# Moving the second layer's modulation into the first group's mixing, and giving each mixing step pairs of picks by its stage

## The chip, the cores and the metric

One core of a Trainium2 chip runs the whole inference step in one launch. The metric is the device time of the launch in microseconds (us), median of the runs. Engines are named as in the profile: PE (matmul), PEld (its weight load), DVE (vector), ACT (scalar), POOL (here it only issues the gathers), SP (here it only issues the loads of weights and states).

## The reference

The trunk has two layers over 640 tokens of width 1024 (512 prompt tokens of one sequence, 8 streams of 16 tokens), float32 throughout. Each layer is:

```
mod = silu(c) @ w_mod + b_mod            # 9 conditioning rows (1 prompt, 8 streams), 1024 x 6144 per layer
sh1, sc1, g1, sh2, sc2, g2 = split(mod, 6)
h = rmsnorm(x, ln1_w) * (1 + sc1) + sh1
x = x + g1 * token_mixer(h)              # input projection, SSD scan, RG-LRU, merge, output projection
h = rmsnorm(x, ln2_w) * (1 + sc2) + sh2
x = x + g2 * peer(h)                     # 8 heads x top 16 = 128 experts for each token
```

`peer` picks for each token 128 of 16384 experts by product keys. Each expert is a row u (1024) and a row v (1024): `gelu(u . h) * gate` weights v. So every token needs 128 gathered rows of 8 KB. The modulation depends on the conditioning vectors alone, and layer 1's is first used when layer 1's first normalised input is modulated.

## The kernel before, in words

**Tokens, tiles and groups.** The 640 tokens are 5 tiles of 128. A layer's mixing runs over two groups: tiles 0 to 2 (N = 384 columns) and tiles 3, 4 (N = 256, with the 8 streams). Layer and group make a region r = 0 to 3. A region's mixing is a list of steps i in stages, `bases` gives where each begins: N1 (norm, 12 steps), X (13), S (SSD scan, 19 or 15), Z (8), LX (9), LRU (8), M (merge, 33), OUT (18, with the second norm), Q (queries, key scores and the choice of experts, 21). In a step of X, Z, LX, LRU, M, OUT or Q, PE projects one tile of weights (512 KB, 90 a region, `project`, L460) through 4 slots `wslot` that SP fills in order (`load`, L331). SP waits with each load until the projection that last read the slot is done (`projected`).

**Picks and pairs.** The experts of a tile are gathered one pick at a time: for pick k, POOL gathers a row of 2048 numbers for each of the 128 tokens (1 MB) into one of the 8 places of `ring` (L447). DVE takes the dot product with u (L1726, `dots`), ACT the gelu (L1202), DVE the weight (L1733), ACT a diagonal matrix of the weights (L1182), and PE adds v by that matrix into PSUM (L858, `values`). The place is free when PE is done (`used`). Two picks are a pair, 64 pairs a tile, 640 pairs for the 10 tiles of both layers. The ring holds 4 pairs.

**The plan.** `plan` writes the order of all of it by hand, as a list of slots: a slot is a pair (or none) and the mixing steps that come behind it on PE and DVE (ACT takes the first step ahead of the pair's work). Every engine works through the same list in order. Region 0 has nothing beside it up to step 7 of Q. Then 28 pairs of tile 0 run two to a step, in its Q. `window(pairs, steps, at, till)` lays a region's steps beside the pairs of the layer or group before, evenly: from pair `at` to pair `till` each pair has the same number of steps. Window 1 has region 1 beside the last 36 pairs of tile 0 and those of tiles 1 and 2 (164 pairs, till 151), window 2 has region 2 beside tiles 3 and 4 (128 pairs, steps from 9 to 122), window 3 has region 3 beside tiles 5 to 7 (192 pairs, 9 to 180), and the last 128 pairs have the final norms. With s a tile of a group that already has its scores, `choose` makes the choice for tile s + 1 in 24 pairs of tile s (one of three pieces a pair; the three hold 14 operations over 256 columns for each head).

**Modulation.** A layer's modulation is 12 chunks of 512 columns (2 MB of `w_modt` each). For a chunk PE makes 16 matmul instructions in four column groups (L496), ACT copies the result to `mod_row` (L943), PE turns and sums it (8 instructions, L507), DVE adds the bias into `modE` (L1299). Layer 0's twelve chunks run in N1 and X of region 0, each loaded in one piece to a quarter of the still empty ring (`mod_chunk`). Layer 1's twelve run as a stage MOD of 16 steps at the end of region 1, in window 1, each loaded as four pieces through the four `wslot` slots. PE's chunk there ends with `projected` + 4, so the loads of the next chunk start after it. PE waits for layer 1's modulation (`mod_row`, `mod_add` 24) at the first SSD tile of region 2.

Of the kernel before, what the change touches and what calls it, by code (L numbers as in the profile page):

```python
# [10 lines left out]
DEPTH, D, P = 2, 1024, 128  # L11
# [40 lines left out]
def bases(g):  # L52
    b = {"N1": 0, "X": 12}
    b["S"] = b["X"] + 13
    b["Z"] = b["S"] + (19 if g == 0 else 15)
    b["LX"] = b["Z"] + 8
    b["LRU"] = b["LX"] + 9
    b["M"] = b["LRU"] + 8
    b["OUT"] = b["M"] + 33
    b["Q"] = b["OUT"] + 18  # L60
    b["MOD"] = b["Q"] + 21
    return b
# [3 lines left out]
LENGTH = [BASE[r]["MOD"] + (16 if r == 1 else 0) for r in range(REGIONS)]  # L66
FINAL = 8


def plan():  # L70
# [25 lines left out]
    window(fresh + pairs_of(1, 2), steps_of(1), 0, 64 - 28 + 115)  # L96
# [14 lines left out]
def weight_positions():  # L111

    pos, n = {}, 0
    for r in range(REGIONS):
# [3 lines left out]
        if r == 1:  # L118
            pos[r, "MOD"] = n
            n += 48  # L120
# [51 lines left out]
def build(nc, a):  # L172
    ctx = ExitStack()
    with ctx:
# [143 lines left out]
        mod_row = room(RM - 512, 512)  # L318
# [3 lines left out]
        with nc.Block() as block:  # L322
            @block.sync
            def _(sp):
# [45 lines left out]
                for r in range(REGIONS):  # L370
# [10 lines left out]
                    for j in range(4):  # L381
                        load(tile(l, TZ + j))
                    if g:
                        states(l)
                    for j in range(4, 8):
                        load(tile(l, TZ + j))
# [12 lines left out]
                    if r == 1:  # L399
# [52 lines left out]
            def _(pe):  # L452
# [28 lines left out]
                def modulation(c, in_ring):  # L481

                    if c:
                        pe.wait_ge(S["mod_row"], c)
                    if in_ring:
                        pe.wait_ge(mod_in[c % 4], 16 * (c // 4 + 1))
                    else:
                        for i in range(4):
                            ready(POS[1, "MOD"] + (c - 12) * 4 + i)
                    for kk in range(2):  # L490
                        for q in range(4):
                            if in_ring:
                                w = mod_slab[:, c % 4, (2 * q + kk) * 512:(2 * q + kk + 1) * 512]
                            else:
                                w = wslot[:, (POS[1, "MOD"] + (c - 12) * 4 + q) % SLOTS, kk * 512:(kk + 1) * 512]
                            last = pe.matmul(bank(5)[32 * q:32 * q + 32, :], cT[:, 2 * q + kk, :], w, start=kk == 0, stop=kk == 1)  # L496
                    if in_ring:
                        last.then_inc(S["mod_main"], 1)
                    else:
                        last.then_inc(projected, 4)  # L500

                def modulation_sum(c):
# [3 lines left out]
                    for d in range(4):  # L506
                        last = pe.matmul(bank(6)[:, d * 9:d * 9 + 9], mod_row[:, d * P:(d + 1) * P], pick32[:, 0:9], start=True, stop=True)  # L507
# [59 lines left out]
                def ssd_tile(r, u, i):  # L567
# [7 lines left out]
                    if i == 1:  # L575
# [242 lines left out]
                def mix(r, i):  # L818
# [4 lines left out]
                    if r == 0 and 2 <= i < 6:  # L823
                        modulation_sum(i - 2)
                    if r == 0 and i < 4:
                        modulation(i, True)
                    x_stage(r, i - b["X"])
                    if r == 0 and 2 <= i - b["X"] < 10:
                        modulation_sum(2 + i - b["X"])
                    if r == 0 and 0 <= i - b["X"] < 8:  # L830
                        modulation(4 + i - b["X"], True)
# [8 lines left out]
                    if r == 1 and 2 <= i - b["MOD"] < 14:  # L840
                        modulation_sum(10 + i - b["MOD"])
                    if r == 1 and 0 <= i - b["MOD"] < 12:
                        if i == b["MOD"]:
                            pe.wait_ge(S["p0"], chosen(2))
                        modulation(12 + i - b["MOD"], False)
# [61 lines left out]
            def _(act):  # L907
# [26 lines left out]
                def modulation(c):  # L934
                    if c < 12:
                        act.wait_ge(S["mod_main"], c + 1)
                    else:
                        act.wait_ge(projected, POS[1, "MOD"] + 4 * (c - 11))
# [4 lines left out]
                    act.activation(mod_row, bank(5), ACT.Copy).then_inc(S["mod_row"], 1)  # L943
# [213 lines left out]
                def mix(r, i):  # L1157
# [4 lines left out]
                    if r == 0 and 1 <= i < 5:  # L1162
                        modulation(i - 1)
                    x_stage(r, i - b["X"])
                    if r == 0 and 1 <= i - b["X"] < 9:
                        modulation(3 + i - b["X"])
# [707 lines left out]
```

## Time and profile before

| what | value |
|---|---|
| median of 3 runs | 4863.31 us (4852.66 to 4869.21) |
| the profiled execution's own time | 4843.43 us |
| its span | 4841.7 us |
| mean granted TensorE clock | 0.865 |
| busy share of the span: PE, DVE, ACT, POOL | 76%, 63%, 24%, 30% |
| moved by DMA | 1609 MB, 1342 MB of it by the gathers, mean 332 GB/s |
| first gather issued | 595.4 us |

Slots of the plan are found in the trace by the dot products, four instruction records to a pair (two products, two reads of the accumulator). Region 0 runs to about 783 us, the last part of it beside pairs; window 1 from 783 to 2006 us, window 2 to 3010, window 3 to 4210, and the last pairs to the end. In a table by stretches the number behind each busy time (x...) counts instructions.

| stretch, us | stages | pairs |
|---|---|---|
| 783 to 1016 | region 1: N1, X, S | 39 |
| 1016 to 1222 | Z, LX, LRU | 25 |
| 1222 to 1424 | M | 32 |
| 1424 to 1532 | OUT | 18 |
| 1532 to 1700 | Q | 21 |
| 1700 to 2006 | MOD (16 steps), then pairs alone | 38 |
| 2006 to 2238 | region 2: N1, X, S | 35 |
| 2238 to 2422 | Z, LX, LRU | 20 |
| 2422 to 2643, 2643 to 2740 | M, OUT | 26, 15 |
| 2740 to 2930, 2930 to 3010 | Q, pairs alone | 17, 15 |
| 3010 to 3289 | region 3: N1, X, S | 49 |
| 3289 to 3532 | Z, LX, LRU | 32 |
| 3532 to 3781, 3781 to 3907 | M, OUT | 41, 22 |
| 3907 to 4096, 4096 to 4210 | Q, pairs alone | 27, 21 |

### The profile page before, as it was taken

To read this page: it belongs to the slowest core of one execution; us is meant where nothing else is said; L and a number is where in the kernel's file an instruction comes from. 1 tells how busy PE (TensorE), PEld (TensorE's weight loads), DVE (VectorE), ACT (ScalarE), POOL (GpSimd) and SP (SyncE) were. 2 spreads that over 40 slices of the span, in tenths; PEclk is the share of its full clock that TensorE was granted. 3 is DMA by queue.
4 is the path that set the end of the run, shared out by engine and by line. 5 is a ranking of instruction groups with operands and counts; after the bars stand their busy time and mean duration, and the time that the engine had idled before them with its cause. 6 is when DMAs were issued, how large, how long until landed. Compare 5 with 4: busy or idle time off the path is not lost. (4 is left out here: it accounts for less than half of the span.)

```text
span 4841.7 us, 54018 instructions
## 1 busy us (share of the span) xinstructions
PE 3687.0 (76%) x19330; PEld 1806.0 (37%) x19330; DVE 3049.1 (63%) x8043; ACT 1145.8 (24%) x3125; POOL 1450.5 (30%) x1298
## 2 busy tenths in 40 slices
PE   7999875888987645689999875778788776555555
PEld 4555531444554311144544331334445432111111
DVE  2460289879645923686843596875974478585554
ACT  2150122324212211223411221241431122121111
POOL 0000033332334212423222313343233333444443
PEclk9999987989998867789999987898899887778877
DMA  7133399999999778988888968999999998999997
GB/s 284 48 100 103 102 356 372 379 381 356 378 414 396 295 287 361 387 302 336 310 322 328 346 227 344 369 415 374 356 374 419 401 391 307 398 404 421 407 421 322
DMA packets 275545, 1609.12 MB, mean 332 GB/s; under 512 B 47514, under 2 KB 52432, under 8 KB 109772
## 3 DMA queue, kind: packets, MB, share of 16 engines
q0 software_dynamic: 184320, 1342.26, 69.6%
q1 hardware_dynamic: 70992, 255.49, 14.3%
q10 hardware_dynamic: 19964, 7.91, 0.6%
q8 instruction: 153, 2.51, 0.2%
q14 instruction: 116, 0.95, 0.1%
HBM read 1597.63 MB, written 7.91 MB: 332 GB/s over the span
## 5 line engine op out<-in xcount | busy, mean ns | idle before, releaser
L447 POOL DMA_INDIRECT ring<-in_peer_uv,eidx x1280 | 1447.3, 1131 | 3355.5 <-PE psum L858 2593.3
L858 PE MATMUL psum<-ring,diag 64*64 64x512 f32 x10240 | 1587.5, 748 | 946.6 <-ACT diag L1182 888.9
L1726 DVE SCALAR_TENSOR_TENSOR ring<-ring,hrow 128x1024 f32<-128x1024 f32 x1280 | 1547.4, 1223 | 1077.4 <-DMA ring<-in_peer_uv,eidx 1069.1
L460 PE MATMUL psum<-hT,wslot 128*128 128x384 f32 (+1 forms) x4224 | 1224.4, 445 | 0.5 <-DMA wslot<-in_w_tiles 0.5
L858 PEld LDWEIGHTS psum<-ring,diag 64*64 64x64 f32 x10240 | 389.8, 157 | 1928.9 <-ACT diag L1182 1351.4
L460 PEld LDWEIGHTS psum<-hT,wslot 128*128 128x128 f32 x4224 | 809.3, 195 | 485.8 <-issue 167.7
L1202 ACT ACTIVATE gel<-hid 128x2 f32<-128x2 f32 x640 | 129.6, 202 | 2195.9 <-DVE ring L1726 2154.5
L460 PE MATMUL psum<-region,wslot 128*128 128x384 f32 (+1 forms) x1536 | 436.8, 438 | 2.1 <-DVE region L1555 1.3
L1182 ACT ACTIVATE diag<-ident,wgt 128x64 f32<-128x64 f32 x1280 | 366.1, 333 | 0.6
L460 PEld LDWEIGHTS psum<-region,wslot 128*128 128x128 f32 x1536 | 287.4, 191 | 170.0 <-issue 52.7
L1733 DVE TENSOR_TENSOR wgt<-gel,gate 128x2 f32<-128x2 f32 x640 | 100.2, 157 | 49.5 <-ACT gel L1202 25.3
L1202 ACT ACT_TABLE_LOAD x84 | 107.8, 1283 | 2.1 <-ACT region L1101 0.7
L496 PE MATMUL psum<-wslot,cT 128*32 128x512 f32 x192 | 42.5, 1032 | 85.4 <-DMA wslot<-in_w_modt 85.4
L1726 DVE DVE_READ_ACCUMULATOR ring<-ring,hrow 128x1 f32 x1280 | 105.7, 83 | 0.0
L1093 ACT ACTIVATE region<-psum 128x384 f32<-128x384 f32 (+1 forms) x64 | 27.7, 433 | 314.6 <-PE psum L460 314.4
L1552 DVE SCALAR_TENSOR_TENSOR region<-region,psum 128x384 f32<-128x384 f32 (+1 forms) x32 | 15.5, 484 | 125.6 <-PE psum L460 125.6
L1337 DVE SCALAR_TENSOR_TENSOR region<-region,vec 128x384 f32<-128x384 f32 (+1 forms) x144 | 81.4, 565 | 5.1
L1546 DVE SCALAR_TENSOR_TENSOR region<-region,psum 128x384 f32<-128x384 f32 (+1 forms) x32 | 15.5, 484 | 88.9 <-PE psum L460 64.1
L1532 DVE RECIPROCAL region<-region 128x384 f32<-128x384 f32 (+1 forms) x32 | 68.7, 2145 | 0.0
L943 ACT ACTIVATE region<-psum 128x512 f32<-128x512 f32 x24 | 14.3, 597 | 221.3 <-PE psum L507 139.2
L1332 DVE COPY carry<-region 128x3 f32<-128x3 f32 x36 | 6.2, 173 | 92.6 <-ACT region L955 71.0
L1579 DVE MAX8 best<-psum 128x8 f32<-128x128 f32 x160 | 39.6, 289 | 34.2 <-PE psum L794 30.3
(255 smaller groups left out, 2818.3 us busy)
## 6 DMA issues: line engine op xcount, KB each, us to landing
wslot<-in_w_tiles SPq DMA_DIRECT2D x360, 512.0 KB
ring<-in_w_modt SPq DMA_DIRECT2D x12, 2048.0 KB, 19.5
wslot<-in_w_modt SPq DMA_DIRECT2D x48, 512.0 KB
ring<-in_peer_uv,eidx POOLq DMA_INDIRECT x1280
wslot<-in_w_gate SPq DMA_DIRECT2D x32, 128.0 KB
region<-in_states_t SPq DMA_DIRECT2D x16, 256.0 KB
region<-in_states_n SPq DMA_DIRECT2D x16, 256.0 KB
out_new_ssd_sample<-region ACTq DMA_DIRECT2D x16, 256.0 KB, 17.4
```

Of the source, the lines that this page charges most:

```text
L447: pool.indirect_dma_start(ring[:, n, :], None, table, bass.IndirectOffsetOnAxis(ap=eidx[:, s % 3, k:k + 1], axis=0))\
L460: last = pe.matmul(out, wslot[:, n % SLOTS, k * P:(k + 1) * P], src(k), start=k == 0, stop=k == KT - 1)
L496: last = pe.matmul(bank(5)[32 * q:32 * q + 32, :], cT[:, 2 * q + kk, :], w, start=kk == 0, stop=kk == 1)
L858: last = pe.matmul(psum[c * H:(c + 1) * H, q, :], diag[rows, n, :], ring[rows, n, D + c * 512:D + (c + 1) * 512], start=k == 0, stop=k == ...
L1093: act.activation(lay.gates[:, q, :], bank(3 + 2 * q)[:, 0:lay.N], ACT.Tanh, scale=0.5).then_inc(S["mg"], 1)
L1182: act.activation(diag[:, pick % RING, :], ident64[:], ACT.Copy, scale=wgt[:, pick % 16:pick % 16 + 1])\
L1202: act.activation(gel[:, v], hid[:, v], ACT.Gelu_apprx_tanh).then_inc(E["gelu"], 1)
L1337: st(dve.scalar_tensor_tensor(y, x[:, k:k + NY], w(k), y, ALU.mult, ALU.add))
L1532: st(dve.reciprocal(lay.rec, lay.rec))
L1579: st(dve.max(vals[:, i, 0:8], src[:, i, :]))
L1726: dve.scalar_tensor_tensor(out=ring[:, n, 0:D], in0=ring[:, n, 0:D], scalar=1.0, in1=hrow[:, s % 2, :], op0=ALU.mult, op1=ALU.mult, accum_ ...
L1733: dve.tensor_tensor(wgt[:, v], gel[:, v], gate[:, s % 3, :, :].rearrange("p h k -> p (h k)")[:, 2 * p:2 * p + 2], ALU.mult)\
```

## The change

Two things are changed.

**The modulation of layer 1** leaves the end of region 1. Its chunks 12 to 23 run in region 0, one a step from Z's first step on (`MOD_AT`: Z has 8 steps, so the last four stand in LX), and are loaded through the empty ring as layer 0's are. `mod_row` lies at another place of `region` for them, over the B and C columns of the convolved input, which the SSD scan has read by then: hence PE and ACT wait at chunk 12 for the scan's last state (`state`). The wait for `mod_row` and `mod_add` 24 moves to the first step of region 0's LRU, and ACT's first merge gate of region 0 waits for `mod_sum` 24. SP issues chunks 12 to 15 behind the X tiles and 16 to 23 one behind a tile of Z or LX.

**The plan's windows** give a step a share by its stage instead of the same to each, and window 1's steps reach to pair 161 instead of 151.

```diff
-LENGTH = [BASE[r]["MOD"] + (16 if r == 1 else 0) for r in range(REGIONS)]
+LENGTH = [BASE[r]["END"] for r in range(REGIONS)]
+MOD_AT = {**{c: c for c in range(4)}, **{BASE[0]["X"] + c: 4 + c for c in range(8)}, **{BASE[0]["Z"] + c: 12 + c for c in range(12)}}
+SHARE = {"N1": 4, "X": 14, "S": 10, "Z": 18, "LX": 17, "LRU": 25, "M": 17, "OUT": 10, "Q": 24}
+def share(r, i):
+    if r >= REGIONS:
+        return 1
+    return SHARE[max((BASE[r][name], name) for name in SHARE if BASE[r][name] <= i)[1]]
...
     def window(pairs, steps, at, till):
-        n, done = len(steps), 0
+        total, past, n = sum(share(*s) for s in steps), 0, 0
         for q, pair in enumerate(pairs):
-            want = 0 if q < at else min(n, -(-n * (q - at + 1) // (till - at)))
-            out.append((pair, steps[done:want]))
-            done = want
-        assert done == n
+            first = n
+            while n < len(steps) and (q + 1 >= till or (past + share(*steps[n]) / 2) * (till - at) <= total * (q + 1 - at)):
+                past += share(*steps[n])
+                n += 1
+            out.append((pair, steps[first:n]))
+        assert n == len(steps)
...
-    window(fresh + pairs_of(1, 2), steps_of(1), 0, 64 - 28 + 115)
+    window(fresh + pairs_of(1, 2), steps_of(1), 0, 64 - 28 + 125)
...
-        mod_row = room(RM - 512, 512)
+        def mod_row(c):
+            return room(RM - 512 if c < 12 else 8 * NG[0], 512)
...  # SP
+                    if r == 0:
+                        for c in range(12, 16):
+                            mod_chunk(c)
+                    for j in range(8):
+                        if g and j == 4:
+                            states(l)
                         load(tile(l, TZ + j))
+                        if r == 0 and j >= 4:
+                            mod_chunk(12 + j)
                     for j in range(8):
                         load(tile(l, TLX + j))
+                        if r == 0 and j < 4:
+                            mod_chunk(20 + j)
-                    if r == 1:
-                        for c in range(12):
-                            for i in range(4):
-                                load(a["w_modt"].rearrange("l c p k -> p (l c) k")[:, 12 + c, i * D:(i + 1) * D])
...  # PE
+                    if c == 12:
+                        pe.wait_ge(S["state"], at("state", 0, 3))
...  # PE, ssd_tile
-                            if r == 2:
-                                pe.wait_ge(S["mod_row"], 24)
-                                pe.wait_ge(S["mod_add"], 24)
...  # PE, lru_stage
+                            if r == 0:
+                                pe.wait_ge(S["mod_row"], 24)
+                                pe.wait_ge(S["mod_add"], 24)
...  # PE, mix
+                    if r == 0 and i - 2 in MOD_AT:
+                        modulation_sum(MOD_AT[i - 2])
+                    if r == 0 and i in MOD_AT:
+                        modulation(MOD_AT[i])
                     ssd_stage(r, i - b["S"])
                     z_stage(r, i - b["Z"])
...  # ACT
                     if c == 12:
-                        act.wait_ge(written, 256)
+                        act.wait_ge(S["state"], at("state", 0, 3))
...  # ACT, merge_stage
+                        if r == 0 and i == 1:
+                            act.wait_ge(S["mod_sum"], 24)
```

## Rows read from the trace of the kernel before

**Rows 1.** The page's part 3: the gathers' queue, its packets, MB, share of 16 engines.
```profile
q0 software_dynamic: 184320, 1342.26, 69.6%
```
**Rows 2.** Dot products (L1726) alone, by stretches: DVE busy (instructions), clock, DMA share, GB/s.
```profile
1700.00:1880.00 180.00, 35.50 (x58) 0.67 0.77 295
...
4600.00:4800.00 200.00, 98.75 (x160) 0.75 1.01 421
```
**Rows 3.** Window 1 by stretches: PE, PEld, DVE, ACT, POOL busy; clock, DMA share, GB/s.
```profile
783.00:1016.00 233.00, 176.71 (x1274) 85.70 (x1266) 203.41 (x518) 82.11 (x238) 91.74 (x78) 0.84 0.97 386
1016.00:1222.00 206.00, 177.26 (x915) 106.75 (x916) 175.83 (x480) 72.43 (x187) 58.46 (x54) 0.91 0.93 357
1222.00:1424.00 202.00, 181.40 (x1037) 112.58 (x1039) 104.00 (x238) 41.36 (x132) 66.97 (x62) 0.98 0.99 401
1424.00:1532.00 108.00, 81.11 (x456) 39.52 (x452) 60.79 (x135) 22.45 (x74) 41.85 (x36) 0.85 0.97 390
1532.00:1700.00 168.00, 122.06 (x660) 72.01 (x656) 145.04 (x562) 43.02 (x105) 46.55 (x42) 0.85 0.85 323
```
**Rows 4.** The modulation of layer 1: PE in order of time (start us, us, ...).
```profile
1703.47 2.44 PE L496 MATMUL psum<-wslot,cT 128*32 128x512 f32 x16
1705.85 1.95 PE L858 MATMUL psum<-ring,diag 64*64 64x512 f32 x16
...
1864.34 3.64 PE L496 MATMUL psum<-wslot,cT 128*32 128x512 f32 x16 [6.88 <-DMA wslot<-in_w_modt]
```
**Rows 5.** Waits of 1700 to 1905: us in total, times, longest.
```profile
PE psum L496 <- DMA wslot<-in_w_modt: 85.4, 11, 12.7
```
**Rows 6.** Region 0, in order of time: two chunks of modulation, the start of Z.
```profile
97.16 1.92 PE L496 MATMUL psum<-ring,cT 128*32 128x512 f32 x16 [0.74 <-ACT region L943]
...
104.28 0.96 PE L507 MATMUL psum<-pick,region 128*128 128x9 f32 x8
...
105.98 1.92 PE L496 MATMUL psum<-ring,cT 128*32 128x512 f32 x16 [0.75 <-ACT region L943]
...
191.63 10.59 PE L460 MATMUL psum<-hT,wslot 128*128 128x384 f32 x32
192.84 0.69 DVE L1434 TENSOR_TENSOR stT<-stT,psum 128x512 f32<-128x512 f32 x1
```
**Rows 7.** Region 0 by stretches: X and S, then Z and LX.
```profile
56.00:191.00 135.00, 121.75 (x661) 67.05 (x662) 71.13 (x129) 26.04 (x51) 0.00 (x0) 0.95 0.29 102
191.00:280.00 89.00, 89.00 (x278) 52.30 (x275) 35.39 (x66) 13.46 (x26) 0.00 (x0) 1.00 0.26 85
```
**Rows 8.** Groups of DVE instructions: one operation of the choice (busy us, mean ns).
```profile
L1582 DVE FIND_INDEX8 pl<-sv,cand 128x8 uint32<-128x256 f32 x80 | 33.5, 419 | 0.0
```
**Rows 9.** Window 2 by stretches, columns as in rows 3.
```profile
2006.00:2238.00 232.00, 194.27 (x1085) 90.67 (x1081) 205.02 (x479) 85.53 (x190) 77.61 (x68) 0.86 0.88 333
2238.00:2422.00 184.00, 184.00 (x777) 92.16 (x774) 127.73 (x234) 72.06 (x145) 48.85 (x43) 1.00 0.86 312
2422.00:2643.00 221.00, 219.41 (x940) 109.58 (x942) 88.28 (x178) 31.34 (x103) 57.69 (x52) 1.00 0.86 323
2643.00:2740.00 97.00, 80.44 (x384) 34.89 (x380) 48.96 (x95) 22.33 (x64) 34.25 (x30) 0.92 0.92 356
2740.00:2930.00 190.00, 142.21 (x644) 72.50 (x640) 159.49 (x672) 41.63 (x93) 33.02 (x34) 0.86 0.67 244
```
**Rows 10.** Window 3 by stretches, columns as in rows 3.
```profile
3010.00:3289.00 279.00, 203.69 (x1422) 94.81 (x1426) 225.12 (x555) 89.32 (x265) 112.03 (x95) 0.85 0.97 393
3289.00:3532.00 243.00, 187.17 (x988) 107.23 (x980) 188.38 (x496) 72.72 (x200) 72.19 (x66) 0.87 0.94 357
3532.00:3781.00 249.00, 209.90 (x1190) 123.19 (x1194) 132.27 (x303) 52.82 (x167) 87.97 (x80) 0.92 0.99 406
3781.00:3907.00 126.00, 95.11 (x540) 42.62 (x536) 70.50 (x155) 24.22 (x86) 52.17 (x46) 0.85 0.99 403
3907.00:4106.00 199.00, 140.33 (x792) 76.67 (x788) 164.62 (x602) 47.84 (x129) 64.12 (x58) 0.83 0.86 333
```

More of the change, by code:

```diff
@@ L60, in bases @@
     b["Q"] = b["OUT"] + 18
-    b["MOD"] = b["Q"] + 21
+    b["END"] = b["Q"] + 21
     return b
 BASE = [bases(r % 2) for r in range(REGIONS)]
-LENGTH = [BASE[r]["MOD"] + (16 if r == 1 else 0) for r in range(REGIONS)]
+LENGTH = [BASE[r]["END"] for r in range(REGIONS)]
 FINAL = 8
+MOD_AT = {**{c: c for c in range(4)}, **{BASE[0]["X"] + c: 4 + c for c in range(8)}, **{BASE[0]["Z"] + c: 12 + c for c in range(12)}}
[4 more added lines that the diff above has]
+    return SHARE[max((BASE[r][name], name) for name in SHARE if BASE[r][name] <= i)[1]]
 def plan():
@@ L479, in norm, with modulation @@
                               .then_inc(S["n_sum"], 1)
-                def modulation(c, in_ring):
+                def modulation(c):
+                    if c == 12:
+                        pe.wait_ge(S["state"], at("state", 0, 3))
                     if c:
                         pe.wait_ge(S["mod_row"], c)
[L485 to L489, printed above, removed]
+                    pe.wait_ge(mod_in[c % 4], 16 * (c // 4 + 1))
                     for kk in range(2):
                         for q in range(4):
[L492 to L495, printed above, removed]
+                            w = mod_slab[:, c % 4, (2 * q + kk) * 512:(2 * q + kk + 1) * 512]
                             last = pe.matmul(bank(5)[32 * q:32 * q + 32, :], cT[:, 2 * q + kk, :], w, start=kk == 0, stop=kk == 1)
[L497 to L500, printed above, removed]
+                    last.then_inc(S["mod_main"], 1)
                 def modulation_sum(c):
@@ L506, in modulation_sum @@
                     for d in range(4):
-                        last = pe.matmul(bank(6)[:, d * 9:d * 9 + 9], mod_row[:, d * P:(d + 1) * P], pick32[:, 0:9], start=True, stop=True)
+                        last = pe.matmul(bank(6)[:, d * 9:d * 9 + 9], mod_row(c)[:, d * P:(d + 1) * P], pick32[:, 0:9], start=True, stop=True)
                     last.then_inc(S["mod_sum"], 1)
@@ L839, in mix @@
                     q_stage(r, i - b["Q"])
[L840 to L845, printed above, removed]
                 def values(pair):
@@ L934, in modulation @@
                 def modulation(c):
[L935 to L938, printed above, removed]
+                    act.wait_ge(S["mod_main"], c + 1)
                     if c:
@@ L941, in modulation @@
                     if c == 12:
-                        act.wait_ge(written, 256)
-                    act.activation(mod_row, bank(5), ACT.Copy).then_inc(S["mod_row"], 1)
+                        act.wait_ge(S["state"], at("state", 0, 3))
+                    act.activation(mod_row(c), bank(5), ACT.Copy).then_inc(S["mod_row"], 1)
                 def fill(r, j, xpad):
@@ L1161, in mix @@
                     norm(2 * r, i, N1_SQ, N1_MEAN)
-                    if r == 0 and 1 <= i < 5:
-                        modulation(i - 1)
                     x_stage(r, i - b["X"])
-                    if r == 0 and 1 <= i - b["X"] < 9:
-                        modulation(3 + i - b["X"])
+                    if r == 0 and i - 1 in MOD_AT:
+                        modulation(MOD_AT[i - 1])
                     ssd_stage(r, i - b["S"])
@@ L1173, in mix @@
                     q_stage(r, i - b["Q"])
-                    if r == 1 and 1 <= i - b["MOD"] < 13:
-                        modulation(11 + i - b["MOD"])
                 def diagonals(n):
@@ L1699, in mix @@
                     norm(2 * r, i, N1_MEAN)
-                    if r == 0 and 3 <= i < 7:
-                        modulation(i - 3)
                     x_stage(r, i - b["X"])
-                    if r == 0 and 3 <= i - b["X"] < 11:
-                        modulation(1 + i - b["X"])
+                    if r == 0 and i - 3 in MOD_AT:
+                        modulation(MOD_AT[i - 3])
                     ssd_stage(r, i - b["S"])
@@ L1712, in mix @@
                     q_stage(r, i - b["Q"])
-                    if r == 1 and 3 <= i - b["MOD"] < 15:
-                        modulation(9 + i - b["MOD"])
                 def dots(s, p):
```

16 lines of the change are left out of this document (removed).

## The prediction, made before the change was run

> **What bounds the kernel now.** I read the page's parts 1 and 3 first. No engine is near full over the span (PE, the fullest, has 76%), and the gathers alone are 1342 MB [rows 1]. So I looked at where pairs go slowly, by counting the dot products of a stretch (four records to a pair) [rows 2]. With hardly any mixing beside them (4600 to 4800 us) 160 records are 40 pairs in 200 us: 5.0 us a pair, at 421 GB/s and a DMA share of 1.01. That is the transfers' own pace, and nothing can put 640 pairs through faster. A tile of weights (0.52 MB) takes the same engines 1.25 us at that rate. The rule "5.0 a pair and 1.25 a tile" gives 32 x 5.0 + 32 x 1.25 = 200 us for region 1's merge, and it took 202 [rows 3]: that stage is bound by the transfers. The other stages of windows 1 to 3 are read in [rows 3, 9, 10], by whichever of three is fullest. In region 2's Z to M, PE is busy 184 of 184 and 219 of 221 us. In Q it is DVE (145 of 168, 159 of 190, 165 of 199), and DMA falls to 323, 244 and 333 GB/s. In N1, X and S it is DVE again (203 of 233, 205 of 232, 225 of 279). And at 1700 to 1880 it is none of them: PE half idle, DVE at a fifth, 58 records = 14.5 pairs in 180 us, 295 GB/s [rows 2]. There PE waits for weights of the modulation, 85 us in 11 waits [rows 5], and chunk follows chunk at (1864.34 - 1703.47) / 11 = 14.6 us [rows 4]: a chunk's four pieces are asked for only when the chunk before has been read, and PE, standing in order, holds back the pair behind it, so the ring.
>
> **The modulation that leaves window 1.** MOD and the pairs alone behind it take 306 us for 38 pairs (783 to 2006 is 1223, less the five stretches of [rows 3] with 917). At 5.0 a pair 38 pairs are 190. So the stage costs 116 us, of which 107 lie in 1700 to 1880 (180 less 14.5 x 5.0). All of it goes: no other work of the slots was late. Its 25 MB go from the busiest DMA time too, which is within the 116.
>
> **What it adds in region 0.** Nothing but PE counts there: Z and LX have PE busy 89 of 89 us, at a granted clock of 1.0, while DMA has a share of 0.26, DVE 35 us and ACT 13 [rows 7]. So every us of PE is paid in full. In X of region 0 a step with one projection, one chunk and one sum takes 105.98 - 97.16 = 8.82 us; two projections of Z alone take 10.59, 5.3 each [rows 6]. The difference, 3.5 us, holds the chunk (1.92), the sum (0.96) and the turn by way of ACT's copy (the 0.74 in brackets). Twelve times 3.5 is 42. The new wait at chunk 12 stands ahead of Z's first projection in PE's queue: the scan's last state is written at 192.84 + 0.69 = 193.5, and PE started that projection at 191.63, so 1.9 more. DVE's and ACT's share (0.6 us of copy and a few small operations a step) hides behind PE. Loads: a step takes 0.5 + 2.1 MB in 9 us, 290 GB/s, below the 421 that the engines do; chunks 12 to 15 are asked for in X and have all of S to come, each later one is asked for three to four steps ahead of its use. SP's tile loads now queue behind 2 MB pieces, and each tile is still wanted only three steps later. The new waits at LRU's first step and at the first merge gate come four steps and more after the last sum: nothing. I take 45 us. Bounds: 35 (twelve times 1.92 + 0.96, no turn, no wait) and 175 (twelve times the 14.6 of [rows 4], nothing hidden).
>
> **What the shares move.** Working the rule of the change through gives each stage's pairs. A pair that leaves or joins a stage is worth what the full engine spends on it: DVE 2.6 us (98.75 / 40 = 2.5 for the products [rows 2], and the small operation for the weight), 2.0 more where a piece of the choice for the next tile goes with it (14 operations of 0.42 in three pairs [rows 8]); PE 2.0 (1.95 at full clock [rows 4]); the transfers 5.0. So a gain comes where a pair leaves a stage full of transfers or of engine work and joins one where transfers had room.
>
> Window 1, now 1223 us [rows 3]. N1, X, S: 39 pairs become 29. DVE 203 - 10 x 2.6 = 177; transfers 29 x 5.0 + 10 tiles = 158. At nine tenths DVE: 197. Z, LX, LRU: 25 become 38. Transfers 38 x 5.0 + 24 x 1.25 + 12 for states and gate weights (5 MB) = 232; DVE 176 + 13 x 2.6 + 6 = 216, at today's fill of 0.85 it would be 254. I take 250, nearer to the second since LRU alone is DVE's. M: 32 become 42, 42 x 5.0 + 40 = 250. OUT: 18 become 14, 80 by the rule and 8 on top as now (100 by the rule, 108 measured): 88. Q: 21 become 38, transfers 210, DVE 145 + 17 x 2.6 = 189; with both so near, 221. Pairs alone: 12 at 5.3 (now 306 - 180 = 126 us for 38 - 14.5 pairs) = 63. Sum 1069: 154 less, of which 116 are the modulation and 38 the shares.
>
> Window 2, now 1004 us [rows 9]. N1, X, S: 35 become 22. PE 194 - 26 = 168, DVE 205 - 34 - 6 = 165; at today's fill of 0.88, 190. Region 0 bears that out: X and S take 135 us with no pair [rows 7], less 8 x 3.5 of modulation is 107, 22 pairs at 2.6 make 164, and N1's chain is some 25 more. Z, LX, LRU: 20 become 26, PE full, 184 + 12 = 196. M: 26 become 29, 227. OUT: 15 become 10, PE 80 - 10 = 70 at its 0.83, 84. Q: 17 become 26; DVE is full and DMA at 244 GB/s, so 9 pairs cost only their dot products, 190 + 22 = 212. Pairs alone, 15 as before, 80. Sum 989: 15 less.
>
> Window 3, now 1200 us [rows 10]. N1, X, S: 49 become 31, DVE 225 - 47 = 178, at nine tenths 198. Z, LX, LRU: 32 become 40, transfers 200 + 30 + 12 = 242, DVE 193; 252. M: 41 become 45, 225 + 40 = 265, 268 (now 249 where the rule gives 245). OUT: 22 become 15, 85 by the rule, 92. Q: 27 become 40, transfers 220, DVE 165 + 34 = 199; 230. Pairs alone as before, 104. Sum 1144: 56 less.
>
> The final norms move by one slot: nothing. Together: -154 - 15 - 56 + 45 = -180. The profiled execution took 4843.43, so 4663. The median of the runs shown is 19.9 above that one, so **4683 us**.
>
> **A rule weighed.** The stretches beside mixing reach 401 and 406 GB/s and the last ones 421 [rows 2, 3, 10]. The Trainium skill (DMA: Bandwidth & Descriptors, "Where 436 GB/s comes from") says that for transfers between HBM and SBUF the HBM side, about 358 GB/s for a core, is what binds. By it, an estimate from that page, a pair would take 5.9 us and window 1's transfers 1160, so the change would have little left to win beyond the modulation. The trace disagrees in every row named.
>
> **Rivals.** *Shares worth nothing.* The slots are bound by the sum of steps and pairs and not by their order; then only the modulation counts, -116 + 45: 4772, with the runs' offset 4792. For it: window 2 has PE full through Z to M whatever the order. Against: DMA at 244 and 323 GB/s in Q, where a pair costs half. Chance 0.10. *Full balance.* DVE and transfers overlap nearly wholly in the new slots; window 1 goes to 1020 (its transfers: 173 x 5.0 + 90 x 1.25 + 12 = 989), window 2 to 960, window 3 to 1110 (1084): -203 - 44 - 90 + 45 = -292, 4551, with offset 4571. For it: M of windows 1 and 3 is within 2% of the rule. Against: four stages run 5 to 10% above it. Chance 0.14. *Bunched steps.* N1's 12 steps now fall into 3 or 4 slots (up to five in one) and S and X often have two; in a slot PE, ACT and DVE hand each other the parts of one norm, and nothing of a pair goes between. If the three stretches N1 to S keep their times though they lose 41 pairs, 36 + 42 + 81 = 159 of the gain go: 4822, with offset 4842. For it: DVE there is at 0.88 and not 1.0. Against: region 0's 135 us without a pair. Chance 0.07. *A capped mix.* Transfers of gathers, weights and states together stay at the 357 GB/s of 1016 to 1222: window 1 with 416 MB takes 1165 (-58), window 3 stays, -58 - 15 + 45: 4815, with offset 4835. Against it, 401 GB/s in M with 32 tiles. Chance 0.03. The page weighed above (DMA: Bandwidth & Descriptors, of the Trainium skill) gives nearly this cap. *Slower: uncovered loads.* In region 0's Z and LX each chunk's 2 MB come one behind the other with the weight tiles behind them on SP's queue, and PE waits as it does in MOD: 175 us, and the shares bring nothing: -116 + 175 = +59, 4902, with offset 4922. It decides from 116 / 12 = 9.7 us for a chunk. For it: that is how the same bytes behave now. Against: four quarters of the ring, and X of region 0 holds 8.82 with the same bytes. Chance 0.03.
>
> **How the numbers follow.** The forecast has 0.63. Its own range is 4630 to 4745: half of each "taken" surplus either way. The range for all is 4590 to 4790: below it lies most of full balance, above it the uncovered loads, the two cases at 4835 to 4842 and half of the first rival. A change under 0.3% (15 us) can't be told from none. Faster by more: 0.63 + 0.10 + 0.14 + 0.07 + part of the cap, 0.95; same 0.02; slower 0.03.
>
> **What would show it.** L496 has two groups in the ring and none in wslot, the second with steps of 8.8 to 9.4 us between 193 and 310 us, no wait for DMA; the first gather is issued about 45 us later, near 640. From there window 1 takes about 1070 us with no stretch under 340 GB/s. Q of window 2 shows DMA at 300 or more against 244. I am wrong if region 0 grows by over 60, if N1's slots hold DVE idle for more than a few us, or if Q's stretches grow by 5 us for each pair that they gain in window 2.

## The result, and the profile after

The changed kernel took 4791.55 us (median of 4 runs, 4790.19 to 4804.21) beside 4860.19 of the kernel before (4 runs): a ratio of 0.9864, 95% interval 0.9839 to 0.9888. It is faster by 69 us where 180 were forecast, and lies 1.6 us outside the stated range. Its profiled execution took 4792.62 us (span 4790.9), so the two profiled executions differ by 50.8, and the account below is of these. (The kernel before was profiled in an execution 17 us quicker than its median, the changed kernel in one 1 us above its own.)

For the account, a stretch runs from the dot product of the first pair in its first slot to that of the next stretch. "Forecast" is the sum in the prediction.

| stretch | before | forecast | after |
|---|---|---|---|
| region 0 up to window 1 | 783.4 | +45 | 835.2 (+51.8) |
| window 1: N1 to S, pairs 39 -> 29 | 232.3 | 197 | 200.3 |
| Z to LRU, 25 -> 38 | 206.6 | 250 | **279.0** |
| M, 32 -> 42 | 201.7 | 250 | 256.5 |
| OUT, 18 -> 14 | 107.8 | 88 | 83.5 |
| Q, 21 -> 38 | 168.1 | 221 | **237.3** |
| MOD and pairs alone, 38 -> 12 | 305.9 | 63 | 68.8 |
| window 2: N1 to S, 35 -> 22 | 232.4 | 190 | 202.6 |
| Z to LRU, M, OUT | 183.9, 220.8, 96.7 | 196, 227, 84 | 196.7, 226.3, 79.2 |
| Q and pairs alone, 32 -> 41 | 270.2 | 292 | 291.4 |
| window 3: N1 to S, 49 -> 31 | 279.4 | 198 | 203.4 |
| Z to LRU, 32 -> 40 | 242.6 | 252 | **276.5** |
| M, OUT | 248.8, 126.3 | 268, 92 | 268.1, 92.9 |
| Q, 26 -> 40 | 186.3 | 230 | **247.9** |
| pairs alone, 22 -> 21 | 116.4 | 104 | 114.3 |
| windows 1, 2, 3 | 1222.4, 1004.1, 1199.8 | 1069, 989, 1144 | 1125.4, 996.3, 1203.1 |
| to the end | 632.0 | 632 | 630.9 |

Where a stage was left with fewer pairs, the forecast was near (N1 to S and OUT, but for 13 us in N1 to S of window 2). In two of the three windows it was wrong for the stages that were given more, Z to LRU and Q.

The modulation first. The page of the changed kernel, part 6: what is loaded, by which queue, how often, KB each, us to landing.

```profile
ring<-in_w_modt SPq DMA_DIRECT2D x24, 2048.0 KB, 9.0
```

All 24 chunks go through the ring. Region 0 of the changed kernel in order of time (start us, us, engine, line), where Z begins.

```profile
193.17 0.69 DVE L1429 TENSOR_TENSOR stT<-stT,psum 128x512 f32<-128x512 f32 x1
193.91 1.92 PE L509 MATMUL psum<-ring,cT 128*32 128x512 f32 x16 [1.89 <-DVE stT L1429]
195.77 5.43 PE L478 MATMUL psum<-hT,wslot 128*128 128x384 f32 x16
...
208.24 0.95 PE L517 MATMUL psum<-pick,region 128*128 128x9 f32 x8
...
209.95 1.92 PE L509 MATMUL psum<-ring,cT 128*32 128x512 f32 x16 [0.75 <-ACT region L940]
```

PE waits 1.89 us for the scan's last state, as forecast (1.9), then each step has chunk, projection and sum with the same 0.75 us for ACT's copy as in X [rows 6]. By the starts of their first projections, Z to LRU took 191.6 to 331.1 us before and 195.8 to 380.1 now, so M begins 49.0 us later; forecast 45. The rest of the 51.8 comes behind it; in the other runs with this region 0 window 1 begins between 832 and 838.5 us, so 3 us of it are within what one trace can tell. PE's waits over 193 to 335 us (us in total, times, longest) name no load, and the second is one that the forecast had put at nothing, a sum of LX that waits 2.5 us for DVE:

```profile
PE psum L509 <- ACT region L940: 7.5, 10, 0.7
PE psum L517 <- DVE modE L1294: 2.5, 1, 2.5
PE psum L509 <- DVE stT L1429: 1.9, 1, 1.9
```

Then window 1 of the changed kernel by stretches, columns as in [rows 3].

```profile
835.00:1035.00 200.00, 151.51 (x1109) 80.06 (x1101) 178.10 (x466) 73.44 (x204) 67.40 (x58) 0.85 0.89 348
1035.00:1314.00 279.00, 210.52 (x1115) 116.10 (x1115) 214.05 (x566) 81.92 (x227) 86.45 (x79) 0.87 0.91 350
1314.00:1571.00 257.00, 214.98 (x1235) 124.32 (x1230) 126.09 (x276) 50.31 (x165) 93.59 (x84) 0.93 1.00 408
1654.00:1892.00 238.00, 159.12 (x928) 81.08 (x920) 188.10 (x648) 52.66 (x153) 80.16 (x75) 0.83 0.94 372
```

Read against the prediction's terms: DVE in Z to LRU is busy 214 us (216 said) and in Q 188 (189 said). DVE's work was summed rightly. But in both stretches neither DVE nor the transfers is full: 0.77 and 0.91 in the first, 0.79 and 0.94 in the second. M answers to the 202 us row of [rows 3]: the DMA share is 1.00 (0.99 there), and the time 6 us above the rule.

What DVE waited for in Z to LRU and in Q of that window (us in total, times, longest):

```profile
DVE ring L1717 <- DMA ring<-in_peer_uv,eidx: 52.6, 24, 5.6
```

```profile
DVE ring L1717 <- DMA ring<-in_peer_uv,eidx: 41.1, 25, 3.0
```

In the kernel before these waits for gathers were 16.8 and 15.0 us. In window 3 they went from 30.5 to 67.5 and from 21.0 to 48.1.

Four stretches of the other windows of the changed kernel: N1 to S and Z to LRU of window 2, then Z to LRU and Q of window 3.

```profile
1961.00:2163.00 202.00, 167.22 (x889) 84.30 (x885) 172.68 (x408) 66.29 (x141) 49.75 (x44) 0.86 0.70 258
2163.00:2360.00 197.00, 192.91 (x843) 94.18 (x840) 143.87 (x271) 77.03 (x164) 61.10 (x52) 0.99 0.92 342
...
3160.00:3437.00 277.00, 212.41 (x1159) 117.72 (x1159) 191.74 (x469) 84.38 (x235) 93.47 (x84) 0.89 0.96 371
...
3798.00:4046.00 248.00, 167.05 (x968) 83.55 (x960) 192.38 (x657) 53.90 (x159) 84.24 (x79) 0.82 0.92 365
```

The second row is Z to LRU of window 2: with PE full (193 of 197) a pair more costs its 2 us of PE and no more (196.7 us, 196 said). The first has lost 13 pairs and its DMA share fell from 0.88 [rows 9] to 0.70: the transfers' room that the shares make there is simply left empty.

What happens in a slot of Q can be read one level down. Region 3, DVE's dot products around one odd step of Q (the choice runs from 3955.9 to 3965.1), then POOL's gathers and PE in the same time.

```profile
3951.11 1.23 DVE L1717 SCALAR_TENSOR_TENSOR ring<-ring,hrow 128x1024 f32<-128x1024 f32 x1
...
3954.65 1.23 DVE L1717 SCALAR_TENSOR_TENSOR ring<-ring,hrow 128x1024 f32<-128x1024 f32 x1 [2.31 <-DMA ring<-in_peer_uv,eidx]
...
3965.07 1.22 DVE L1717 SCALAR_TENSOR_TENSOR ring<-ring,hrow 128x1024 f32<-128x1024 f32 x1
```

```profile
3960.63 0.93 POOL L465 DMA_INDIRECT ring<-in_peer_uv,eidx  x1 [2.70 <-PE psum L858]
3961.87 0.94 POOL L465 DMA_INDIRECT ring<-in_peer_uv,eidx  x1 [0.30 <-issue]
3970.26 0.94 POOL L465 DMA_INDIRECT ring<-in_peer_uv,eidx  x1 [7.45 <-PE psum L858]
```

```profile
3958.74 1.95 PE L858 MATMUL psum<-ring,diag 64*64 64x512 f32 x16
3967.97 3.63 PE L858 MATMUL psum<-ring,diag 64*64 64x512 f32 x16 [7.29 <-ACT diag L1177]
```

DVE waits 2.31 us for a gather, then stands 9 us in the choice. PE waits 7.29 us for the diagonals, which need weights that DVE makes only behind the choice and the next pair's products; POOL waits 7.45 us for PE, and issues nothing from 3962 to 3970. Seven products later DVE waits for a gather again, 2.52 us at 3979.72. The ring holds four pairs, but two of them are in the hands of DVE, ACT and PE, so gathers are at most two pairs, some 10 us, ahead.

The idle time also slows PE. Its granted clock is 1.00 over 3950 to 3960 us and 0.57 over 3968 to 3972, behind 8 us in which it was busy 0.7 us, and the 16 instructions that took 1.95 us before the wait take 3.63 after it. So the places come back another 1.7 us later. No run separates this from the wait itself.

### The profile page after: what moved, and what is told of

The parts are those of the page before. It is cut to its first block and busy times, and to the rows that moved or that the text cites. A ratio compares the mean times of both kernels' runs of the same rounds, so it can differ in the third digit from the quotient of the medians.

```text
span 4790.9 us, 53957 instructions
## 1 busy us (share of the span) xinstructions
PE 3664.5 (76%) x19330; PEld 1810.3 (38%) x19330; DVE 3047.8 (64%) x8043; ACT 1133.9 (24%) x3117; POOL 1436.0 (30%) x1298
## 5 line engine op out<-in xcount | busy, mean ns | idle before, releaser
L465 POOL DMA_INDIRECT ring<-in_peer_uv,eidx x1280 | 1432.8, 1119 | 3315.8 <-PE psum L858 2495.5
L858 PE MATMUL psum<-ring,diag 64*64 64x512 f32 x10240 | 1567.6, 740 | 954.1 <-ACT diag L1177 895.1
L478 PE MATMUL psum<-hT,wslot 128*128 128x384 f32 (+1 forms) x4224 | 1240.8, 449 | 5.7 <-DMA wslot<-in_w_tiles 5.7
L1547 DVE SCALAR_TENSOR_TENSOR region<-region,psum 128x384 f32<-128x384 f32 (+1 forms) x32 | 15.5, 485 | 106.9 <-PE psum L478 106.9
L1469 DVE SCALAR_TENSOR_TENSOR region<-region,psum 128x384 f32<-128x384 f32 (+1 forms) x32 | 15.5, 484 | 96.9 <-ACT region L1038 96.9
L1541 DVE SCALAR_TENSOR_TENSOR region<-region,psum 128x384 f32<-128x384 f32 (+1 forms) x32 | 15.5, 485 | 91.3 <-PE psum L478 70.6
L1560 DVE SCALAR_TENSOR_TENSOR xT<-psum,modE,xT 128x384 f32<-128x384 f32 (+1 forms) x32 | 15.4, 483 | 89.8 <-PE psum L478 89.8
L509 PE MATMUL psum<-ring,cT 128*32 128x512 f32 x384 | 47.5, 614 | 31.5 <-DMA ring<-in_w_modt 16.0
```

The costliest lines, as they stand in the source:

```text
L465: pool.indirect_dma_start(ring[:, n, :], None, table, bass.IndirectOffsetOnAxis(ap=eidx[:, s % 3, k:k + 1], axis=0))\
L478: last = pe.matmul(out, wslot[:, n % SLOTS, k * P:(k + 1) * P], src(k), start=k == 0, stop=k == KT - 1)
L858: last = pe.matmul(psum[c * H:(c + 1) * H, q, :], diag[rows, n, :], ring[rows, n, D + c * 512:D + (c + 1) * 512], start=k == 0, stop=k == ...
L1469: st(dve.scalar_tensor_tensor(lay.zt, lay.zth[:, j % 2, :], 1.0, bank(3 + j % 2)[:, 0:lay.N], ALU.add, ALU.mult))
```

## The experiments

Each was timed against the kernel before on the same chip in three rounds (ratio with its 95% interval), but two that were run once for their trace. The chips differ, so runs of different series are compared by ratio, and stretches by their traces. A trace is one execution: Z to LRU of region 3 under the same plan took 242.6, 239.4 and 245.9 us in three of them (before, experiments 1 and 2), so a few us in one stretch tell nothing.

**1. The modulation moved, the shares left out.** Window rule and lengths of the kernel before.

```diff
-    window(fresh + pairs_of(1, 2), steps_of(1), 0, 64 - 28 + 125)
+    window(fresh + pairs_of(1, 2), steps_of(1), 0, 135)      # and window() as in the kernel before
```

> Layer 1's modulation in region 0 as in the changed kernel, but the windows of the kernel before: every step of a window the same share, window 1's 137 remaining steps up to pair 135, which is where they ended before. Short-lead theory (two of the ring's four pairs are always held by DVE, ACT and PE, so transfers are at most two pairs ahead; a long slot idles them whatever its neighbours are, and moving pairs between stages gains nearly nothing): windows 2 and 3 as in the kernel before (1004 and 1200 us), window 1 1223 - 116 = 1107, region 0 +52 as in the changed kernel's trace: 4863 - 64 = about 4799, the same as the changed kernel within 10. Rival, shares gain what was forecast but bunched steps lose it again in the changed kernel: also about 4799 here, but then the stretches N1 to S alone must be what is long in the changed kernel. Rival, the shares do gain in sum: this one is 20 us or more slower than the changed kernel, 4812 or more.

4790.73 us beside 4848.97, 0.9872 (0.9849 to 0.9894). The changed kernel has 0.9864. So nearly the whole gain is the modulation's, and the shares are worth nothing that can be measured. In the trace window 1 takes 1115.8 us (1222.4 before, so -107 where -116 was forecast), and windows 2 and 3 take 1006.0 and 1199.0. By the traces the windows of the changed kernel (shares, and window 1 reaching to pair 161) differ from these by +10, -10 and +4 us. N1 to S is not what is long in the changed kernel (forecast 197, 190, 198, measured 200.3, 202.6, 203.4), which speaks against bunched steps as the cause.

**2. Even steps up to pair 161.** The edit is against experiment 1.

```diff
-    window(fresh + pairs_of(1, 2), steps_of(1), 0, 135)
+    window(fresh + pairs_of(1, 2), steps_of(1), 0, 64 - 28 + 125)
```

> As the one before it, but window 1's 137 even steps reach to pair 161, as in the changed kernel. Short-lead theory: window 1 changes by under 15 us, since a pair is worth about 5 us anywhere except in slots where DVE is far over 5 us. Theory that a pair in a stage bound by DVE or PE costs only 2.0 to 2.6 us: the 25 more pairs beside steps save 2.4 us each in the stages bound by engines, about 30 to 40 us, 4760.

4778.86 us, 0.9852 (0.983 to 0.9875), window 1 at 1101.9 us. 26 slots that held a pair alone now hold steps, for 14 us: 0.5 us each, near the "under 15" of the short lead and far from the 30 to 40. Against this plan, which has the same end, the shares cost window 1 23 us (1125.4). By the times alone (0.9852, 0.9864) the two can't be told apart.

**3. The first of the choice's three pieces moved from Q's odd steps to its even ones**, on the changed kernel.

```diff
                                 best_keys(s + u, j, score(j, u))
+                            choose(s, j, 1)
                         else:
                             best_keys(s + 1, j, score(j, 1))
-                            for piece in (1, 2, 3):
+                            for piece in (2, 3):
```

> The changed kernel with the first piece of the choice moved from the odd to the even steps of Q, so that DVE's work in a step of window 1 and 3 is about 6 and 6 us and not 3.6 and 9. The DVE work is the same. Short-lead theory: the odd slots, 14 us now with 11.5 of work, lose the wait; a cycle of two steps with four pairs goes from 25 to 22.5 us, seven cycles in windows 1 and 3 each: 35 us less in all, window 2's Q (DVE full) the same within 5; about 4756. Rival, DVE and transfers add up in Q by contention and not by order: the same within 5.

4777.49 us, 0.9843 (0.9818 to 0.9869); the interval overlaps the changed kernel's, so the effect is read from the traces. The slots of Q's odd steps in region 1 go from 13.2 to 9.8 us on average, those of the even steps from 6.1 to 9.1. The gain is there but smaller than expected: Q of window 1 falls from 237.3 to 228.9 us and of window 3 from 247.9 to 237.3, 19 us together and not 35, and window 2 loses (its Q and the pairs behind, 291.4 to 296.8). Q of window 1 in this run, columns as before:

```profile
1650.00:1879.00 229.00, 159.86 (x932) 81.87 (x928) 187.84 (x647) 53.74 (x156) 80.42 (x75) 0.87 0.97 384
```

The same DVE work (187.8 us) in other portions, and the DMA share rises from 0.94 to 0.97. Half of what Q took beyond the forecast goes by order alone (8 of 16 and 11 of 18 us), which refutes contention as the whole cause.

**4. Weights and diagonals of the last pair ahead of this pair's work**, on the changed kernel.

```diff
 # DVE, pair(s, p); ACT likewise: diagonals(n) ahead of the gelu
+                    n = s * PAIRS + p - 1
+                    if 0 <= n < TILES_E * PAIRS:
+                        weights(n)
                     if s < TILES_E:
                         dots(s, p)
-                    n = s * PAIRS + p - 1
-                    if 0 <= n < TILES_E * PAIRS:
-                        weights(n)
```

> The changed kernel with each engine's part of a pair turned round: DVE makes the weights of the last pair ahead of this pair's dot products, and ACT makes the last pair's diagonal matrices ahead of this pair's gelu. A ring place is then free one pair of dot products (2.5 us) and its wait for the gather earlier, and nothing else changes. Short-lead theory: everything bound neither by DVE nor PE alone gains, 40 to 120 us in all, 4670 to 4750. Rival, transfers are slowed by what runs beside them (contention): within 10 us of the changed kernel, 4792. Against it: in slots without mixing DVE now waits for the gelu at once, about 0.5 us in a slot that has slack.

4758.89 us, 0.9807 (0.9785 to 0.983), some 28 us below the changed kernel by the ratios. Less than 40, so the size of the expectation was missed, but no work was removed, and the windows fall by 16, 9 and 7 us. Q goes from 237.3 to 231.3 us in window 1 and from 247.9 to 237.1 in window 3. Z to LRU goes from 279.0 to 269.3 in window 1, where DVE's waits for gathers fall from 52.6 to 39.1 us, but only from 276.5 to 275.4 in window 3. The row of window 1 shows the DMA share up from 0.91 to 0.96:

```profile
1039.00:1308.00 269.00, 208.10 (x1115) 115.46 (x1108) 214.90 (x568) 81.97 (x222) 84.19 (x80) 0.88 0.96 366
```

**5. Gathers of half the bytes**, on the changed kernel, one run.

```diff
-                table = a["peer_uv"].rearrange("l e d -> (l e) d")
+                table = a["peer_uv"].rearrange("l e (h d) -> (l e h) d", h=2)
...
-                        pool.indirect_dma_start(ring[:, n, :], None, table,
+                        pool.indirect_dma_start(ring[:, n, 0:D], None, table,
```

> The changed kernel with gathers of half the bytes: a pick brings one row of 1024 numbers, the v half of a ring place keeps old data (this leaves out half of what the experts need). Engines do the same work in the same order. It shows what each stretch costs without the transfers. Short-lead theory (transfers and DVE are each near full and too short a lead keeps them from overlapping): region 1's Z to LRU, 279 us for 38 pairs, falls to DVE's own 214 to 230; region 1's Q with 38 pairs, 238 us, falls to 190 to 200, its odd slots from 14 to 11.5 us; region 2's Z to M, PE full, stays at 423. Rival, the slots are bound by the hand-over between DVE, ACT and PE in a bunched or empty slot: these stretches keep over 0.9 of their times.

4310.3 us. Z to LRU and Q of region 1, columns as before:

```profile
1022.00:1268.00 246.00, 198.78 (x1101) 110.27 (x1093) 212.91 (x566) 79.37 (x222) 91.59 (x79) 0.90 0.73 234
1550.00:1760.00 210.00, 152.95 (x921) 79.99 (x920) 186.88 (x646) 52.22 (x153) 74.88 (x75) 0.87 0.70 232
```

With transfers at 0.73 and 0.70 these stretches take 246.6 and 210.1 us for 213 and 187 us of DVE work: the expected 214 to 230 and 190 to 200 were both missed, and so was the rival's 0.9 of the old times (both are at 0.88). The odd slots of Q did fall to 11.8 us, near the expected 11.5. DVE's waits in the two stretches:

```profile
DVE ring L1717 <- DMA ring<-in_peer_uv,eidx: 22.0, 13, 4.2
```

```profile
DVE ring L1717 <- DMA ring<-in_peer_uv,eidx: 14.4, 11, 3.6
```

So at half the bytes DVE still waits 22 and 14 us for gathers. Beside the 52.6 and 41.1 of the changed kernel that is 31 and 27 us less, which is the whole fall of the stretches (32 and 27). What is left beyond DVE's work and these waits is 12 and 9 us in this run, 12 and 8 in the changed kernel. So 247 and 210 us are upper bounds of the engines' own time, and the run doesn't say how far below them it lies. In region 3 the same stretches take 229.8 us (276.5) and 217.2 (247.9). The stretches bound by PE in window 2 keep their times, as expected (Z to LRU 196.2, M 226.4 us), and N1 to S of window 2 keeps its 201: DVE waits for no gather there in either kernel, and the forecast 190 was 11 short of the engines' own time.

**6. The stores of the states cut to an eighth**, on the changed kernel, one run.

```diff
-                                act.dma_start(dst[:, l, j, :, :], lay.states[:, (8 + j) % 5, :].rearrange("p (b n) -> p b n", b=STREAMS))\
+                                act.dma_start(dst[:, l, j, 0:1, :], lay.states[:, (8 + j) % 5, 0:NS].rearrange("p (b n) -> p b n", b=1))\
```

> The changed kernel, but the 16 stores of the streams' SSD states in the second group of each layer write one stream of eight (this leaves seven eighths of that output out): 1/8 of the 9376 small packets in each of the two stretches. Theory that the transfers of Z to LRU were underrated because packets of 256 bytes take DMA time far beyond their bytes: the stretches Z to LRU of regions 1 and 3, 279 and 277 us, lose 8 to 15 us each, and DMA share times length there falls by about 12 us. Rival, they are bound by lumps in DVE's slots: under 3 us each.

4781.5 us. Z to LRU takes 270.8 us in region 1 (279.0) and 265.0 in region 3 (276.5): 8.2 and 11.5 less, as expected. DMA share times length falls by 8 (254 to 246) and 12 (266 to 254), where 12 was said for each. The packets can be read in the kernel before: its queue of stores (packets, MB, share of 16 engines) over Z to LRU of region 3, 3289 to 3532 us, then in M right behind it.

```profile
q10 hardware_dynamic: 9376, 2.36, 4.4%
```

```profile
q10 hardware_dynamic: 246, 0.29, 0.3%
```

2.36 MB in packets of some 250 bytes take 0.044 x 243 = 10.7 us of all 16 engines, where 421 GB/s would make it 5.6. The Trainium skill (DMA: Bandwidth & Descriptors, "Why small descriptors are slow (HBM only)") names, as one of two reasons, a fixed cost for each packet, 11 cycles instead of 8 for 256 bytes, which is an estimate of 1.4 times; the trace has 1.9.

**7. The even plan with both edits of order**, and **8. a mixed plan**: the same with window 2 by shares up to pair 126, window 3 even up to pair 189, and the choice split only for groups of two tiles. Here `window` is the even rule of the kernel before and `by_share` that of the changed kernel.

```diff
-    window(pairs_of(3, 4), steps_of(2), 9, 122)
-    window(pairs_of(5, 6, 7), steps_of(3), 9, 180)
+    by_share(pairs_of(3, 4), steps_of(2), 9, 126)
+    window(pairs_of(5, 6, 7), steps_of(3), 9, 189)
...
+                            if lay.nt == 2:
+                                choose(s, j, 1)
```

> Even shares, window 1 up to pair 161, with both edits of order: the first piece of the choice in Q's even steps, and weights and diagonals of the last pair ahead of this pair's products and gelu. Short-lead theory: each gives what it gave on the changed kernel (14 and 33 us there), less in Q since fewer pairs stand in it; 4863 - 72 - 12 - 30 = 4745 to 4755 by the scale of the first series. Rival, both only mended what the shares had done: as even161 within 8 us, 0.985 of before.

> As the one before, but window 2 by shares (it gained 8 to 10 us by them) and reaching to pair 126, window 3 even to pair 189, and the choice split only for groups of two tiles (window 2's Q lost 5 us by it). By the trace of window 1 (14 us for 26 pairs more beside steps) window 3 gains 3 to 6 us, window 2 by shares 10, its longer reach 2 to 5: 15 to 20 us below the one before. Theory that pairs are worth 5 us wherever transfers are near full: window 3 gains under 3, window 2 8 to 12.

The first took 4741.61 us beside 4856.76, 0.9763 (0.9737 to 0.9789), which is 4748 on the scale of its expectation (4863) and lies in it: the edits give as much without the shares. The mixed plan took **4724.0 us, 0.9727 (0.9703 to 0.9751)**, faster than both kernels: 2.7% below the kernel before, twice the gain of the change. By the ratios it is 17 us below the first, as expected in sum. Its windows take 1086.6, 994.6 and 1181.1 us against 1088.7, 1001.1 and 1187.9: window 3 gained 7 where 3 to 6 were said, window 2 only 6 where 12 to 15 were.

**9. The changed kernel with both edits of order.**

> The changed kernel (shares, window 1 to pair 161) with both edits of order. Against the even plan with both edits (4742 us beside a kernel before of 4857, 0.9763) it tells whether the short lead is why the shares gained nothing. If it is the only cause, the shares now pay part of what was forecast: 0.972 or less. If the cause is also that engine time in Z to LRU and Q is 15 and 11% above DVE's busy time whatever the lead (as the run with half the bytes shows), the shares still lose a little: 0.977 to 0.981.

4743.49 us beside 4841.55, 0.9797 (0.9765 to 0.9829), against 0.9763 of the even plan. By the ratios the shares lose 16 us, but the intervals overlap, and by their traces the two are level (spans 4737.5 and 4739.5). It is the expectation's second case, 0.977 to 0.981, and not 0.972. The shares' balance over the three windows goes from +23 - 9 + 4 = +18 us (against experiment 2) to +12 - 10 - 5 = -3. So the longer lead takes away their loss and doesn't turn it into the forecast gain.

## Why the prediction was wrong

**The direction, the place and one of the two parts were right.** The modulation's term held: 116 us were to go from window 1, 107 went (experiment 1); 45 were to come in region 0, 49 came up to M and 52 up to window 1. That alone is the rival "shares worth nothing" (4792 forecast, 4791.55 measured), which had 0.10. Its mechanism was right, but that the number is so near is in part luck: it said 71 us less for the profiled executions, where the changed kernel had 51 less and the one of experiment 1 had 46, and the 19.9 us that it added for the other runs belonged to the kernel before alone (the changed kernel was profiled at 4792.62).

**The step that failed is "what the shares move"**, and in it the value of a pair that joins Z to LRU or Q of a group of two tiles. In window 1 the forecast amounts to 3.3 us for each pair that joins Z to LRU and 3.1 in Q; measured were 5.6 and 4.1. The forecast missed by 109 us in the medians and by 129 in the profiled executions: +29 and +24.5 in Z to LRU of windows 1 and 3, +16 and +18 in their Q, +13 in N1 to S of window 2, +3 and +5 in N1 to S of the others, +7 in region 0, and the rest in small terms, among them 10 in the pairs alone of window 3. That last one is bookkeeping: Q of the kernel before ended at 4093, but 104 us was read from 4106 on, so 12 of its 116 us were counted with Q.

Three things lay behind the large ones, each with a number.

*The transfers of Z to LRU were taken from bytes.* The rule gave 167 and 202 us for the stretches of the kernel before, while its own rows had a DMA share of 0.93 of 206 and 0.94 of 243 us, that is 192 and 228 [rows 3, 10]. 25 us were missing in each, and they could be read from the rows. Of region 3's 26 us, 14 are gathers at 388 instead of 421 GB/s and 5 the stores' packets beyond their bytes (last section). With 13 and 8 pairs at 5.0 more the transfers come to 257 and 268; the changed kernel has 0.91 x 279 = 254 and 0.96 x 277 = 266. The stores' small packets are worth 8 to 12 us of these stretches (experiment 6).

*DVE's waits for gathers grew with the pairs.* Z to LRU of window 1 took 176 us of DVE's work, 17 of waits for gathers and 14 for the rest; now it takes 214, 53 and 12. Q took 145, 15 and 8; now 188, 41 and 8. The prediction had DVE's work right, but allowed 34 us beyond it in Z to LRU and 32 in Q, where 65 and 50 came.

*In Z to LRU and Q, DVE and the transfers don't overlap on a lead of two pairs.* Z to LRU of window 1 had 254 us of transfers, and took 247 at half the bytes, but 279 with both; Q had 224 (0.94 x 238), took 210 at half the bytes, and 237 with both. Experiments 3 and 4 show that order alone moves this: 8 and 11 us in Q of windows 1 and 3 by cutting the choice; 6 and 11 there, 10 and 1 in their Z to LRU and 28 in all by freeing the ring earlier, with unchanged work and bytes. It does not hold for any two resources: M of window 1 had transfers at 1.00 and PE at 0.84 (215 of 257 us) and stayed 6 us above the rule. Why M overlaps and Z to LRU doesn't isn't shown; for Q it is shown that shorter pieces of DVE's work help. How far this goes with a ring of more pairs wasn't tried.

What the shares took from N1 to S they had to give to stages in this state. Window 1 against experiment 1: -32 us there, -25 in OUT and -128 in the pairs alone (26 pairs fewer), against +72 in Z to LRU, +53 in M and +69 in Q, together +10. A pair brought 3.2 us where it left N1 to S and cost 5.6 where it joined Z to LRU. Only window 2 gained (8 to 10 us), where PE is full and transfers have room.

**Other points.** "Full balance" (0.14) was refuted by the same numbers. "Bunched steps" (0.07) can explain 11 to 13 us in window 2 at most. The uncovered loads did not occur: PE waited for no load in region 0's Z and LX. Two of the signs of being wrong did not come: region 0 grew by 52 us and not over 60, and Q of window 2 by 2.3 us a pair and not 5. None had been set on Z to LRU or on Q of windows 1 and 3, where the forecast failed. "A capped mix" did not hold as a rate: M runs at 408 GB/s, and the pairs without mixing at 421 as before. That also stands against the HBM limit of 358 GB/s of the Trainium skill (DMA: Bandwidth & Descriptors, "Where 436 GB/s comes from").

## What to carry to other kernels

Before pairing work by its length, read for each stretch the busy share of every resource that will be near full after the move, DMA included, and not its bytes. Count what the engine at the head of the chain already waits for the ring, and expect that to grow with each pair: here the stretches with DVE at 0.7 to 0.8 and transfers at 0.91 to 0.96 took 1.04 to 1.1 times their transfers' time. A ring's lead is its places less those that its consumers hold, and giving them back earlier took 28 us away here with no work removed. The shares moved the windows by -3 to +18 us in sum, the reach from pair 135 to 161 by -14, and the best plan tried, which also left the choice whole in window 2, by another -17. A stage that loads through narrow slots in order is worth moving to where memory lies idle even if its matmuls are then paid in full (107 us against 52).

## What the runs showed of the hardware that was not expected

Stores in packets of some 250 bytes take 1.9 times the DMA time of their bytes (10.7 us for 2.36 MB).

Gathers of the same 8 KB rows take more DMA time for their bytes in some stretches than in others, and the stores are not the reason. In the kernel before, 69.4 MB took 0.736 x 243 = 179 us in region 3's Z to LRU, 388 GB/s. In M behind it, 83.7 MB took 0.816 x 249 = 203 us, 412 GB/s. With an eighth of the stores (experiment 6) Z to LRU of region 1 has 80.4 MB in 0.764 x 270 = 206 us, 390 GB/s, beside 80.6 MB in 0.736 x 279 = 205 us, 393 GB/s, in the changed kernel. And Q of region 1, which has none of these stores, has 397 GB/s there and 379 in the kernel before. What slows them stays open.

The granted clock fell from 1.00 to 0.57 behind 8 us in which PE was nearly idle, in the middle of a stage, and the 16 instructions behind which a pair's two places are free took 3.63 us where they had taken 1.95.
